# The gates' sigmoid as exp(min(g, 0) - ln(1 + exp(-|g|))) in place of 1 / (1 + exp(-g))

## The chip, the cores and the metric

The kernel runs on one core of one Trainium2 chip. The metric is the device time of one execution in microseconds, all input loads and the output store included. Engines are called as the profile calls them: PE is TensorE (PEld its weight loads), DVE is VectorE, ACT is ScalarE, POOL is GpSimd, SP is SyncE.

## What is computed

A first transformer-like block (Fourier mixing, attention, a gated delta rule, an MLP), and then a second block of two layers. The change lies in the second block's attention, whose core is this:

```
h = x @ w_in[i]                                      # x: 256 tokens x 1024 channels, fp32
(fq, fk, fv, ff_logit, sq, sk, sv, dq, dk, dv, iq, ik, iw, g) = split_cols(h)
o_fox = fox_attention(fq, fk, fv, log_f)             # 6 heads, softmax
o_sb  = stick_breaking_attention(sq, sk, sv)         # 5 heads
o_dsa = dsa_attention(dq, dk, dv, iq, ik, iw)        # 5 heads, softmax over selected keys
gates = jax.nn.sigmoid(g.reshape(b, s, 3, 1024))
merged = (gates[:, :, 0] * (o_fox @ w_up_fox[i])
          + gates[:, :, 1] * (o_sb @ w_up_sb[i])
          + gates[:, :, 2] * (o_dsa @ w_up_dsa[i]))
x = layer_norm(DEEPNORM_ALPHA * x + merged @ w_out[i], ln1_g[i], ln1_b[i])
```

g has 3 x 1024 channels for 256 tokens. Its sigmoid is used only at `merged`, after all heads.

## The kernel before

All products are fp32 on 128 partitions. The second block is a loop over two layers (`second_block`). Each layer is one block of five instruction streams, one per engine, that run in their own written order and meet only at semaphores.

PSUM banks 4 to 7 are used in turn by a list of jobs (`layer_jobs`): job n takes bank 4 + n mod 4, and TensorE may open it once job n - 4 has been read out for the last time. Each job names the engine that gives this last reading ("dve" or "act"). The class `Reader` counts these readings: `open` waits for the job's products (`products_done`), `read` marks the last reading (`dve_emptied` or `act_emptied`). `Writer` does the same on TensorE. `Step` is an engine's wait for its own earlier results.

The order of the attention is written by `attention_schedule()` and followed by all three compute engines. First come eight index heads. Then, for n = 0 to 16, a round of up to four jobs stands: **S** (scores of head n), **T** (of head n - 1: transposed probabilities, or the running sums of a stick-breaking head), **gate n** while n < 12, and **V** (the values' product of head n - 1). Heads 0 to 5 are fox, 6 to 10 stick-breaking (sb), 11 to 15 dsa. So T and V belong to an sb head in the rounds n = 7 to 11, all of which have a gate, and the rounds 12 to 16 have none. As a full round has four jobs, each gate takes the bank of the gate before it.

A gate job is 2 x 8 matmuls of 128x256 with the weights in the ring buffer (line 814), and gives 512 columns: two groups of 128 channels for 256 tokens. The SBUF tensor `sig` holds all twelve.

What the engines do with gate n:

- ScalarE, at gate n: one ACTIVATE from PSUM, exp(-g), into `sig` (line 1086). It is the job's last reading.
- VectorE, at gate n: `sigmoid(n - 1)`, that is 1 + sig (line 1217) and its reciprocal (line 1218) for the gate *before*. The twelfth stands after the last head, ahead of the merge.

In an sb head ScalarE forms ln(1 + exp(-|z|)) by Abs, Exp and Ln (lines 1097, 1099, 1101), VectorE combines it (lines 1246, 1249, 1251), adds T (line 1276), ScalarE takes the Exp (line 1117), and at V VectorE forms the weights (line 1282) before it reads V's product (line 1287). TensorE's V product (lines 969 to 971) waits for these weights (`sb_weights`). In a softmax head VectorE scales and reduces the scores (lines 1258, 1262, 1263), ScalarE takes the Exp and copies T (line 1042), VectorE divides V by its sum (lines 1291, 1292). The selection of keys (lines 1207, 1210) runs on VectorE in the first four fox heads.

After the heads come the transposes of the output (line 979), the up-projections (lines 988 to 995) and the merge on VectorE, which reads `sig` (lines 1305 to 1310).

Of the kernel before, what the change touches and what calls it, by code (L numbers as in the profile page):

```python
# [21 lines left out]
ALU = mybir.AluOpType  # L22
ACT = mybir.ActivationFunctionType
# [262 lines left out]
GATE_JOBS = 12  # L286


def attention_schedule():

    steps = [("idx", str(h)) for h in range(8)]
    last = None
    for n, (kind, h) in enumerate(HEADS + [(None, None)]):
        if kind:
            steps.append(("S", f"{kind}{h}"))
        if last:
            steps.append(("T", last))
        if n < GATE_JOBS:  # L300
            steps.append(("gate", str(n)))
        if last:
            steps.append(("V", last))
        last = f"{kind}{h}"
    return steps


def layer_jobs():
    j = Jobs()
    for c in range(4):  # L310
        j.add(f"xT{c}", "act")
    for n in ("fq01", "fq2fk0"):
        j.add(n, "act")
    j.add("fk12", "dve")
    j.add("ikw", "dve")
    for t in range(TT):
        j.add(f"fv{t}", "dve")
    for n in ("iq01", "iq23"):
        j.add(n, "act")
    for n in ("dq01", "dq2dk"):  # L320
        j.add(n, "act")
    for t in range(TT):
        j.add(f"dv{t}", "dve")
    for n in ("sq01", "sq2sk0", "sk12"):
        j.add(n, "act")
    for t in range(TT):
        j.add(f"sv{t}", "act")
    for n in ("ik", "iq01", "iq23", "dq01", "dq2dk"):
        j.add(f"rot_{n}", "dve")
    j.add("cum", "dve")  # L330
    j.add("cumT", "act")
    for kind, n in attention_schedule():
        j.add(f"{kind}_{n}", {"idx": "act", "gate": "act", "S": "dve", "V": "dve",
                              "T": "dve" if n[:2] == "sb" else "act"}[kind])
    for c in range(4):
        j.add(f"oT{c}", "act")
    for c in range(KC):
        j.add(f"up{c}a", "dve")
        j.add(f"up{c}b", "dve")
    for c in range(4):  # L340
        j.add(f"yT{c}", "act")
    return j


def build(nc, a, out):
# [4 lines left out]
    with ExitStack() as ctx:  # L350
# [35 lines left out]
        def sem(name):  # L386
            return ctx.enter_context(nc.semaphore(name))
# [23 lines left out]
        sb_ln_done, sb_lnot, sb_exp, sb_weights = sem("sb_ln_done"), sem("sb_lnot"), sem("sb_exp"), sem("sb_weights")  # L411
        ik_in, pT_in, bf_in_sem, merged = sem("ik_in"), sem("pT_in"), sem("bf_in"), sem("merged")
        ple_added = sem("ple_added")
        first_sems = [sem(n) for n in ("qk_ready", "g_ready", "conv_ready", "l2_ready", "L_ready", "A_ready", "X_ready",
                                       "vk_ready", "S_zero", "dn_ready", "x1_ready", "gate_in", "conv_out",
                                       "conv_silu", "conv_exp", "e2_done", "decay_in", "decay_done", "pads_zero",
# [7 lines left out]
                     probs_ready, max_ready,  # L424
                     acc_full, out_done, consts_in, hid_full, hid_raw, hid_done, ple_full,
                     ple_exp, ple_read, idx_used, ln_ready, lf_in, lf_ln, lf_ready, sb_ln_done, sb_lnot, sb_exp,
                     sb_weights, ik_in, pT_in, bf_in_sem, merged, ple_added, *first_sems]
        numbers = sorted(s.num for s in loop_sems)
        assert numbers == list(range(numbers[0], numbers[-1] + 1))
        clear = range(numbers[0], numbers[-1] + 1)  # L430
# [248 lines left out]
        def second_block():  # L679
# [8 lines left out]
            sig = carve(24 * SEQ)  # L688
# [49 lines left out]
            with nc.Fori(0, LAYERS) as layer:  # L738
# [11 lines left out]
                with nc.Block() as block:  # L750
# [281 lines left out]
                    def _(act):  # L1032
                        step = Step(act, act_step)
                        r = Reader(act, j2, "act", step)
# [5 lines left out]
                        def copy(name, dst, width=512, scale=None):  # L1040
                            ps = r.open(name, width)
                            ins = act.activation(dst, ps, ACT.Copy) if scale is None else act.mul(dst, ps, scale)  # L1042
                            r.read(name, ins)
# [4 lines left out]
                        ps = r.open("fq2fk0")  # L1048
# [12 lines left out]
                        ps = r.open("dq2dk")  # L1061
# [4 lines left out]
                        ps = r.open("sq2sk0")  # L1066
                        act.mul(sqT[0:HD, 512:768], ps[0:HD, 0:256], 0.125)
                        r.read("sq2sk0", act.activation(skT[:, 0:256], ps[:, 256:512], ACT.Copy))
                        ps = r.open("sk12")
# [4 lines left out]
                        ps = r.open("cumT", 256)  # L1074
                        r.read("cumT", act.activation(cT[0:6, :], ps[0:6, :], ACT.Copy))

                        for kind, name in attention_schedule():
                            if kind == "idx":
                                h = int(name)
                                if h >= 2:  # L1080
                                    act.wait_ge(idx_used, h - 1)
                                r.read(f"idx_{name}", act.activation(rl[h % 2], r.open(f"idx_{name}", 384), ACT.Relu))
                            elif kind == "gate":
                                n = int(name)

                                r.read(f"gate_{n}", act.activation(sig[:, 512 * n:512 * (n + 1)],
                                                                   r.open(f"gate_{n}"), ACT.Exp, scale=-1.0))
                            elif kind == "S":
                                k, h = head(name)[:2]
                                if k == "sb":  # L1090

                                    act.wait_ge(products_done, j2.full(f"S_{name}"))
                                    ps = psum[:, j2.bank(f"S_{name}"), 0:384]
                                    b = sb_ln[h % 2]
                                    if h >= 2:
                                        act.wait_ge(sb_lnot, h - 1)
                                    step(act.activation(b, ps, ACT.Abs))
                                    step.wait()
                                    step(act.activation(b, b, ACT.Exp, scale=-1.0))
                                    step.wait()  # L1100
                                    act.activation(b, b, ACT.Ln, bias=1.0).then_inc(sb_ln_done, 1)
                                else:
                                    i = softmax_heads.index(name)
                                    act.wait_ge(max_ready, i + 1)
                                    if i >= 2:
                                        act.wait_ge(products_done, j2.full(f"T_{softmax_heads[i - 2]}"))
                                    d = 2 * i
                                    act.activation(pr[i % 2][:, 0:P], ts[i % 2][:, 0:P], ACT.Exp,
                                                   bias=nmax[:, d:d + 1], accum_out=den[:, d:d + 1])
                                    act.activation(pr[i % 2][:, P:384], ts[i % 2][:, P:384], ACT.Exp,  # L1110
                                                   bias=nmax[:, d + 1:d + 2],
                                                   accum_out=den[:, d + 1:d + 2]).then_inc(probs_ready, 1)
                            elif kind == "T":
                                k, h = head(name)[:2]
                                if k == "sb":
                                    act.wait_ge(emptied["dve"], j2.emptied(f"T_{name}")[1])
                                    act.activation(sb_arg[h % 2], sb_arg[h % 2], ACT.Exp).then_inc(sb_exp, 1)
                                else:
                                    i = softmax_heads.index(name)
                                    if i >= 2:  # L1120
                                        act.wait_ge(products_done, j2.full(f"V_{softmax_heads[i - 2]}"))
                                    copy(f"T_{name}", pt[i % 2], 384)
                        for c in range(4):
                            copy(f"oT{c}", oT[:, 512 * c:512 * (c + 1)])
                        act.wait_ge(merged, KC)
# [27 lines left out]
                    def _(dve):  # L1153
# [3 lines left out]
                        def do(ins):  # L1157
                            step(ins)
                            step.wait()
# [50 lines left out]
                                    step(dve.match_replace(score[:, at:at + n], best[t], score[:, at:at + n], TAKEN))  # L1210
                                step.wait()

                        def sigmoid(n):

                            r.after(f"gate_{n}")
                            g = sig[:, 512 * n:512 * (n + 1)]
                            do(dve.tensor_scalar(g, g, 1.0, None, ALU.add))
                            step(dve.reciprocal(g, g))  # L1218

                        for kind, name in attention_schedule():  # L1220
                            if kind == "idx":
# [13 lines left out]
                                if h == 7:  # L1235
                                    do(dve.tensor_tensor(score, score, const_a("chunked"), ALU.add))
                            elif kind == "gate":
                                if int(name) > 0:
                                    sigmoid(int(name) - 1)
                            elif kind == "S":  # L1240
                                k, h = head(name)[:2]
                                ps = r.open(f"S_{name}", 384)
# [49 lines left out]
                                    r.read(f"V_{name}", dve.tensor_tensor(dst, v3(ps, HD), spread(rden[:, d:d + 2], HD),  # L1292
                                                                          ALU.mult))
                        step.wait()
                        sigmoid(GATE_JOBS - 1)
                        step.wait()


                        sig4 = sig.rearrange("p (b c t) -> p b c t", b=3, c=KC)
                        for c in range(KC):  # L1300
# [1083 lines left out]
```

## Time and profile before

| | |
|---|---|
| time, median of 3 runs | 1898.52 us (1897.86 to 1905.82) |
| profiled execution: time, span | 1899.21 us, 1897.4 us |
| TensorE busy | 89% of the span, granted clock 0.903 on average |
| VectorE busy | 46%, 871.7 us |
| ScalarE busy | 24%, 458.8 us |
| DMA | 228.75 MB, 121 GB/s on average |

The profile is of one execution, from the hardware's profiler. Its span is the time from the first to the last instruction; the time of the execution holds 1.8 us more. A granted clock of 1.00 is 2.4 GHz, one of 0.50 is 1.2 GHz. The two attention stages, one per layer, lie at about 838 to 991 us and 1432 to 1585 us; the rows below are of the first, and those of the second read alike. An engine's rows are merged where alike instructions follow each other: x32 is 32 records. A matmul in fp32 shows as two records. "[0.28 <-DVE work L1282]" says that the engine was idle for 0.28 us before the row and what ended that.

### The profile page before, as it was taken

What the parts mean: (1) busy time and instruction counts of PE and PEld (TensorE: products, weight loads), DVE (VectorE), ACT (ScalarE), POOL (GpSimd) and SP (SyncE); (2) the same over time, 40 slices, a digit from 0 to 9 for tenths busy, and PEclk for the clock granted to TensorE, in tenths of its full rate; (3) what the DMA queues carried; (4) which work ended last, traced back from release to release, by engine and by line L of the source; (5) the groups of instructions that cost most, each with busy time, mean ns of one, the idle gap of its engine ahead of it and who ended that gap; (6) DMA issues with size and microseconds to landing.
All of it is one profiled execution on the core that took longest, in us unless ns stands there. A gap on an engine that the chain in (4) does not pass through costs nothing. (4 is left out here: it accounts for less than half of the span.)

```text
span 1897.4 us, 22118 instructions
## 1 busy us (share of the span) xinstructions
PE 1690.6 (89%) x8995; PEld 1323.4 (70%) x8995; DVE 871.7 (46%) x1319; ACT 458.8 (24%) x755; POOL 36.8 (2%) x59
## 2 busy tenths in 40 slices
PE   4997989998799979989979899994998988799995
PEld 1555978556499967768865699953776876499982
DVE  0634965333455530047644555543007654455536
ACT  2102232112244420011220344401002221244420
POOL 0002010000000000000000000000000000000000
PEclk7987989675899988989979899996998997999998
DMA  9421110330445216322313454405432231545420
GB/s 361 149 89 46 44 46 1 126 129 13 147 174 200 100 45 208 137 89 89 133 45 119 167 199 179 177 0 180 139 116 89 93 129 45 177 158 196 177 89 22
DMA packets 102156, 228.75 MB, mean 121 GB/s; under 512 B 5441, under 2 KB 13761, under 8 KB 101313
## 3 DMA queue, kind: packets, MB, share of 16 engines
q1 hardware_dynamic: 99056, 219.80, 32.6%
q10 hardware_dynamic: 3024, 7.90, 1.1%
q8 instruction: 54, 0.88, 0.2%
q14 instruction: 22, 0.17, 0.0%
HBM read 226.64 MB, written 1.05 MB: 120 GB/s over the span
## 5 line engine op out<-in xcount | busy, mean ns | idle before, releaser
L814 PE MATMUL psum<-xT,ring 128*128 128x256 f32 (+1 forms) x1504 | 335.8, 386 | 12.9 <-issue 12.9
L814 PEld LDWEIGHTS psum<-xT,ring 128*128 128x128 f32 (+1 forms) x1504 | 273.9, 185 | 66.5 <-issue 18.7
L586 PE MATMUL psum<-channels_rounded,work_rounded 128*128 128x256 f32 x1536 | 284.9, 286 | 2.1 <-DVE work_rounded L654 2.1
L623 DVE TENSOR_TENSOR work_rounded<-ring,work_rounded 128x1024 fp32r<-128x1024 f32 x192 | 222.4, 1220 | 103.9 <-ACT work_rounded L614 103.8
L597 PE MATMUL psum<-work_rounded 128*128 128x512 f32 x1152 | 265.7, 390 | 0.0
L586 PEld LDWEIGHTS psum<-channels_rounded,work_rounded 128*128 128x128 f32 x1536 | 244.9, 195 | 4.8 <-issue 3.9
L597 PEld LDWEIGHTS psum<-work_rounded 128*128 128x128 f32 x1152 | 214.7, 188 | 43.6
L614 ACT ACTIVATE work_rounded<-ring 128x1024 fp32r<-128x1024 f32 x192 | 187.5, 1049 | 176.1 <-PE psum L597 108.3
L586 PE MATMUL psum<-work_rounded 128*128 128x256 f32 x768 | 219.3, 286 | 0.0
L586 PEld LDWEIGHTS psum<-work_rounded 128*128 128x128 f32 x768 | 149.5, 195 | 0.8
L664 DVE TENSOR_TENSOR work<-work 128x512 f32<-128x512 f32 x48 | 33.2, 692 | 110.1 <-ACT work L636 110.1
L1218 DVE RECIPROCAL work<-work 128x512 f32<-128x512 f32 x24 | 80.5, 3354 | 0.8
L1830 ACT ACTIVATE work<-psum 128x512 f32<-128x512 f32 (+1 forms) x65 | 37.5, 577 | 118.1 <-PE psum L1642 85.7
L1042 ACT ACTIVATE work<-psum 128x384 f32<-128x384 f32 (+2 forms) x44 | 22.8, 519 | 174.4 <-PE psum L814 145.5
L636 ACT ACTIVATE work<-psum 128x512 f32<-128x512 f32 x48 | 28.7, 598 | 140.8 <-PE psum L586 140.8
L1498 PE MATMUL psum<-ring,small 128*32 128x512 f32 x192 | 38.2, 939 | 23.8 <-DMA ring<-in_w_mod 23.7
L1001 PE MATMUL psum<-ring,work 128*128 128x512 f32 x128 | 55.5, 594 | 3.0 <-DVE work L1310 3.0
L1027 PE MATMUL psum<-ring,xT 128*128 128x512 f32 x128 | 56.2, 592 | 0.0
L821 PE MATMUL psum<-ring,xT 128*128 128x8 f32 (+3 forms) x256 | 55.1, 369 | 0.0
L821 PEld LDWEIGHTS psum<-ring,xT 128*128 128x128 f32 x256 | 39.8, 196 | 15.4 <-issue 2.3
L666 DVE TENSOR_TENSOR work_rounded<-work,work_rounded 128x512 fp32r<-128x512 f32 x48 | 33.3, 693 | 33.5 <-ACT work_rounded L638 33.5
L1001 PEld LDWEIGHTS psum<-ring,work 128*128 128x128 f32 x128 | 24.2, 190 | 33.5 <-issue 29.7
(353 smaller groups left out, 1969.0 us busy)
## 6 DMA issues: line engine op xcount, KB each, us to landing
ring<-in_w_in SPq DMA_DIRECT2D x22, 2048.0 KB, 8.4
ring<-in_w_ff SPq DMA_DIRECT2D x16, 2048.0 KB, 8.1
ring<-in_w_ff_in SPq DMA_DIRECT2D x16, 2048.0 KB, 7.8
ring<-in_w_ff_out SPq DMA_DIRECT2D x16, 2048.0 KB, 7.8
ring<-in_w_mod SPq DMA_DIRECT2D x12, 2048.0 KB, 8.1
ring<-in_w_out SPq DMA_DIRECT2D x6, 2048.0 KB, 7.9
ring<-in_w_up SPq DMA_DIRECT2D x4, 2048.0 KB, 8.0
ring<-in_w_ple_gate SPq DMA_DIRECT2D x4, 2048.0 KB, 7.8
```

The costliest lines, as they stand in the source:

```text
L586: mm = pe.matmul(psum[:, 4 + 2 * half + q, i * SEQ:(i + 1) * SEQ], w1[pw][:, k, m * P:(m + 1) * P], y[py][:, k, :], start=((k, n) == (0, 0 ...
L597: mm = pe.matmul(psum[:, 2 * t + n, :], h[ph][:, kq, t * P:(t + 1) * P], w2[pw][:, kq, n * 512:(n + 1) * 512], start=False, stop=False, sk ...
L614: act.activation(parts.high[i % 2][:, at], ring[:, SLOT * (n % RING) + 1024 * c: SLOT * (n % RING) + 1024 * (c + 1)], ACT.Copy).then_inc(w ...
L623: dve.tensor_tensor(parts.low[i % 2][:, at], ring[:, SLOT * (n % RING) + 1024 * c: SLOT * (n % RING) + 1024 * (c + 1)], exact(parts.high[i ...
L666: dve.tensor_tensor(parts.h_low[:, 2 * q:2 * q + 2, :], h, exact(parts.h_high[:, 2 * q:2 * q + 2, :]), ALU.subtract).then_inc(hid_done, 1)
L814: mm = pe.matmul(ps[base:base + m, at:at + SEQ], unit[:, k, col:col + m], yT8[:, k, :], start=(k == 0), stop=(k == KC - 1))
L821: mm = pe.matmul(ps[:, at:at + n], yT8[:, k, t * P:(t + 1) * P], unit[:, k, col:col + n], start=(k == 0), stop=(k == KC - 1))
L1001: mm = pe.matmul(psum[:, 2 * t + h, :], mergedT[:, k, t * P:(t + 1) * P], u[:, k, :], start=(k == 0), stop=(k == KC - 1))
L1027: mm = pe.matmul(psum[:, 4 + 2 * t, :], yT8[:, k, t * P:(t + 1) * P], u[:, k, :], start=(k == 0), stop=(k == KC - 1))
L1218: step(dve.reciprocal(g, g))
L1498: mm = pe.matmul(ps[strip, :], cs3[:, k, :], wu[:, k, :], start=(k < 4), stop=(k >= 4))
L1830: r.read(name, act.activation(dst, r.open(name, width), ACT.Copy))
```

## The change

The sigmoid is written as exp(min(g, 0) - ln(1 + exp(-|g|))), which equals 1 / (1 + exp(-g)).

ScalarE takes |g| from PSUM into `sig`, then exp(-|g|) and ln(1 + ...) in place, each behind a wait for the one before. VectorE takes min(g, 0) from PSUM minus that, into `sig`, once `gate_ln` says that the logarithm is there; this is now the job's last reading, so the gate jobs change from "act" to "dve". ScalarE takes the final exp in place one round later (`gate_end`), and `gate_ready` tells VectorE ahead of the merge. The add and the reciprocal go. Per gate ScalarE has four operations where it had one, VectorE one where it had two.

```
-        j.add(f"{kind}_{n}", {"idx": "act", "gate": "act", "S": "dve", "V": "dve",
+        j.add(f"{kind}_{n}", {"idx": "act", "gate": "dve", "S": "dve", "V": "dve",
...
+                        def gate_end(n):
+
+                            g = sig[:, 512 * n:512 * (n + 1)]
+                            r.after(f"gate_{n}")
+                            act.activation(g, g, ACT.Exp).then_inc(gate_ready, 1)
...
                             elif kind == "gate":
                                 n = int(name)
-
-                                r.read(f"gate_{n}", act.activation(sig[:, 512 * n:512 * (n + 1)],
-                                                                   r.open(f"gate_{n}"), ACT.Exp, scale=-1.0))
+                                if n:
+                                    gate_end(n - 1)
+                                g = sig[:, 512 * n:512 * (n + 1)]
+                                step(act.activation(g, r.open(f"gate_{n}"), ACT.Abs))
+                                step.wait()
+                                step(act.activation(g, g, ACT.Exp, scale=-1.0))
+                                step.wait()
+                                act.activation(g, g, ACT.Ln, bias=1.0).then_inc(gate_ln, 1)
...
+                        gate_end(GATE_JOBS - 1)
                         for c in range(4):
                             copy(f"oT{c}", oT[:, 512 * c:512 * (c + 1)])
...
-                        def sigmoid(n):
-
-                            r.after(f"gate_{n}")
+                        def sigmoid_log(n):
+
                             g = sig[:, 512 * n:512 * (n + 1)]
-                            do(dve.tensor_scalar(g, g, 1.0, None, ALU.add))
-                            step(dve.reciprocal(g, g))
+                            ps = r.open(f"gate_{n}")
+                            dve.wait_ge(gate_ln, n + 1)
+                            r.read(f"gate_{n}", dve.scalar_tensor_tensor(out=g, in0=ps, scalar=0.0, in1=g,
+                                                                         op0=ALU.min, op1=ALU.subtract))
...
                             elif kind == "gate":
-                                if int(name) > 0:
-                                    sigmoid(int(name) - 1)
+                                sigmoid_log(int(name))
...
                         step.wait()
-                        sigmoid(GATE_JOBS - 1)
-                        step.wait()
-
+                        dve.wait_ge(gate_ready, GATE_JOBS)
```

Where that puts the instructions, for a round whose T and V are of a stick-breaking head (n = 7, the first of five). On VectorE before, from the add of T (line 1276) over the gate's two operations (1217, 1218) to V's weights (1282), V's copy (1287) and the next head's scores:

```order
L1276 TENSOR_TENSOR work<-work,psum 128x384 [waits dve_emptied,products_done]
L1217 TENSOR_SCALAR work<-work 128x512 [waits act_emptied]
L1218 RECIPROCAL work<-work 128x512 [waits dve_step]
L1282 SCALAR_TENSOR_TENSOR work<-work,shared_consts 128x384 [waits sb_exp]
L1287 COPY work<-psum 128x2x64 [waits products_done,dve_emptied,dve_step]
L1246 SCALAR_TENSOR_TENSOR work<-psum,work 128x384 [waits sb_ln_done,products_done,dve_emptied]
L1249 TENSOR_TENSOR work<-work,shared_consts 128x384 [waits dve_step]
L1251 TENSOR_TENSOR work<-psum,work 128x384
```
On VectorE after, the same stretch; line numbers are those of the changed kernel (1289 is the add of T, 1295 the weights, 1300 V's copy):

```order
L1289 TENSOR_TENSOR work<-work,psum 128x384 [waits dve_emptied,products_done]
L1231 SCALAR_TENSOR_TENSOR work<-psum,work 128x512 [waits gate_ln,products_done,dve_emptied]
L1295 SCALAR_TENSOR_TENSOR work<-work,shared_consts 128x384 [waits sb_exp]
L1300 COPY work<-psum 128x2x64 [waits products_done,dve_emptied]
L1259 SCALAR_TENSOR_TENSOR work<-psum,work 128x384 [waits sb_ln_done,products_done,dve_emptied]
L1262 TENSOR_TENSOR work<-work,shared_consts 128x384 [waits dve_step]
L1264 TENSOR_TENSOR work<-psum,work 128x384
```
In place of the two operations stands one from PSUM (line 1231), which waits for `gate_ln` and for the current gate's products instead of an earlier reading; the weights stand directly behind it.

On ScalarE before, from the Exp of T (line 1117) over the gate's Exp (1086) to the next head's Abs, Exp and Ln:

```order
L1117 ACTIVATE work<-work 128x384 [waits dve_emptied]
L1086 ACTIVATE work<-psum 128x512 [waits products_done,act_emptied]
L1097 ACTIVATE work<-psum 128x384 [waits sb_lnot,products_done]
L1099 ACTIVATE work<-work 128x384 [waits act_step]
L1101 ACTIVATE work<-work 128x384 [waits act_step]
```
On ScalarE after, the same stretch (1129 is the Exp of T, 1082 the final Exp of the gate before, 1095 to 1099 Abs, Exp and Ln of the current gate):

```order
L1129 ACTIVATE work<-work 128x384 [waits dve_emptied]
L1082 ACTIVATE work<-work 128x512 [waits dve_emptied]
L1095 ACTIVATE work<-psum 128x512 [waits products_done]
L1097 ACTIVATE work<-work 128x512 [waits act_step]
L1099 ACTIVATE work<-work 128x512 [waits act_step]
L1109 ACTIVATE work<-psum 128x384 [waits sb_lnot,products_done]
L1111 ACTIVATE work<-work 128x384 [waits act_step]
L1113 ACTIVATE work<-work 128x384 [waits act_step]
```
Four operations stand where one stood. TensorE's order doesn't change; the first matmul of a gate waits for its bank by `dve_emptied` in place of `act_emptied`.

## Rows read from the trace of the kernel before

**Rows 1.** The page: engine shares; costliest groups (busy, mean ns, idle before).

```profile
PE 1690.6 (89%) x8995; PEld 1323.4 (70%) x8995; DVE 871.7 (46%) x1319; ACT 458.8 (24%) x755; POOL 36.8 (2%) x59
...
L1218 DVE RECIPROCAL work<-work 128x512 f32<-128x512 f32 x24 | 80.5, 3354 | 0.8
```
**Rows 2.** Busy time by stretch: PE, PEld, DVE, ACT, POOL; PEclk; DMA share; GB/s.

```profile
862.00:904.00 42.00, 42.00 (x207) 34.63 (x207) 28.50 (x55) 8.42 (x25) 0.00 (x0) 1.00 0.29 100
914.00:962.00 48.00, 46.89 (x236) 40.07 (x235) 31.87 (x39) 12.14 (x25) 0.00 (x0) 1.00 0.25 88
```
**Rows 3.** Timeline of one stick-breaking round (gate 8): start, duration, engine, line.

```profile
923.46 0.49 ACT L1097 ACTIVATE work<-psum 128x384 f32<-128x384 f32 x1 [1.32 <-PE psum L911]
...
923.98 0.52 ACT L1099 ACTIVATE work<-work 128x384 f32<-128x384 f32 x1
...
924.33 7.07 PE L814 MATMUL psum<-xT,ring 128*128 128x256 f32 x32
...
924.54 0.52 ACT L1101 ACTIVATE work<-work 128x384 f32<-128x384 f32 x1
...
925.19 0.56 DVE L1246 SCALAR_TENSOR_TENSOR work<-psum,work 128x384 f32<-128x384 f32 x1 [2.19 <-ACT work L1101]
...
926.84 0.55 DVE L1276 TENSOR_TENSOR work<-work,psum 128x384 f32<-128x384 f32 x1
...
927.77 3.35 DVE L1218 RECIPROCAL work<-work 128x512 f32<-128x512 f32 x1
...
931.04 0.50 DVE L1282 SCALAR_TENSOR_TENSOR work<-work,shared_consts 128x384 f32<-128x384 f32 x1
...
931.50 0.60 ACT L1086 ACTIVATE work<-psum 128x512 f32<-128x512 f32 x1 [3.54 <-PE psum L814]
...
931.68 0.41 PE L969 MATMUL psum<-work 128*128 128x64 f32 x2 [0.28 <-DVE work L1282]
```
**Rows 4.** Groups by line and form, whole execution: count, busy us, mean ns.

```profile
L1920 ACT ACTIVATE work<-work 128x512 f32<-128x512 f32 x8 | 5.0, 630 | 16.6 <-DVE work L2177 16.6
...
L1333 DVE SCALAR_TENSOR_TENSOR x_tok<-x_tok,psum 128x512 f32<-128x512 f32 x8 | 5.5, 688 | 28.0 <-PE psum L1001 28.0
```
**Rows 5.** Timeline: gate 11's end, three rounds of the tail, the merge's start.

```profile
960.90 0.41 PEld L969 LDWEIGHTS psum<-work 128*128 128x128 f32 x2
...
961.38 0.60 ACT L1086 ACTIVATE work<-psum 128x512 f32<-128x512 f32 x1 [5.35 <-PE psum L814]
...
965.58 0.41 PE L969 MATMUL psum<-work 128*128 128x64 f32 x2 [2.36 <-ACT work L1042]
...
970.12 0.66 PE L969 MATMUL psum<-work 128*128 128x64 f32 x2 [2.03 <-ACT work L1042]
...
976.04 0.66 PE L969 MATMUL psum<-work 128*128 128x64 f32 x2 [2.00 <-ACT work L1042]
...
994.66 0.69 DVE L1305 TENSOR_TENSOR work<-psum,work 128x512 f32<-128x512 f32 x1 [3.94 <-PE psum L991]
```
**Rows 6.** Timeline: end of gates 1, 5, 6 and start of 2, 6, 7.

```profile
862.94 0.60 ACT L1086 ACTIVATE work<-psum 128x512 f32<-128x512 f32 x1 [4.74 <-PE psum L814]
...
865.74 0.30 PEld L814 LDWEIGHTS psum<-xT,ring 128*128 128x128 f32 x2
...
903.25 0.60 ACT L1086 ACTIVATE work<-psum 128x512 f32<-128x512 f32 x1 [4.79 <-PE psum L814]
...
904.82 0.30 PEld L814 LDWEIGHTS psum<-xT,ring 128*128 128x128 f32 x2
...
912.10 0.60 ACT L1086 ACTIVATE work<-psum 128x512 f32<-128x512 f32 x1 [5.47 <-PE psum L814]
...
914.26 0.30 PEld L814 LDWEIGHTS psum<-xT,ring 128*128 128x128 f32 x2
```
**Rows 7.** Busy time by stretch around the longest pause before the attention's heads.

```profile
832.40:838.30 5.90, 0.06 (x2) 0.06 (x2) 5.49 (x12) 0.00 (x0) 0.00 (x0) 0.65 0.44 165
838.30:844.20 5.90, 5.90 (x35) 5.07 (x36) 3.00 (x9) 3.04 (x7) 0.00 (x0) 0.50 0.00 0
844.20:850.00 5.80, 5.80 (x28) 4.43 (x26) 5.55 (x18) 2.25 (x7) 0.00 (x0) 0.98 0.00 0
```

More of the change, by code:

```diff
@@ L413, in build @@
         ple_added = sem("ple_added")
+        gate_ln, gate_ready = sem("gate_ln"), sem("gate_ready")
         first_sems = [sem(n) for n in ("qk_ready", "g_ready", "conv_ready", "l2_ready", "L_ready", "A_ready", "X_ready",
@@ L426, in build @@
                      ple_exp, ple_read, idx_used, ln_ready, lf_in, lf_ln, lf_ready, sb_ln_done, sb_lnot, sb_exp,
-                     sb_weights, ik_in, pT_in, bf_in_sem, merged, ple_added, *first_sems]
+                     sb_weights, ik_in, pT_in, bf_in_sem, merged, ple_added, gate_ln, gate_ready, *first_sems]
         numbers = sorted(s.num for s in loop_sems)
```

## The prediction

> **What bounds the kernel now.** I read the engine shares first, then the table by stretch, then the order of time inside one attention round. TensorE is busy in 89% of the span, VectorE in 46%, and the 24 reciprocals that go are 80.5 us of VectorE's time [rows 1]. The stretches say whether those 80.5 us cost anything: in the softmax rounds TensorE is busy 42.00 of 42 us, in the stick-breaking rounds 46.89 of 48, both at full clock [rows 2]. So while the gates run, TensorE is the bound, and a reciprocal is worth only the time by which it makes TensorE wait. A round in time [rows 3] shows how little that is. The 16 gate products (32 records) run from 924.33 for 7.07 us. Beneath them VectorE does the previous head's add (926.84), the gate's add and the reciprocal (927.77), and then the weights of that head's V product (line 1282, from 931.04), which TensorE needs right after the gate. It waits 0.28 us for them. That happens in four rounds a layer, so removing every reciprocal can give back about 8 x 0.28 = 2.2 us.
>
> **What the change does to the order.** It moves the gate's step on VectorE from work on the *previous* gate, done long ago, to work on the *current* gate: VectorE now waits for gate n's products and for three ScalarE operations on them, and only then comes to what stands behind, the previous head's V step. In the rounds n = 7 to 11 that step begins with the weights (line 1282 before, 1295 after), and TensorE's V product, next in its queue after gate n, waits for them. Before, they were made under the gate's products. Now they can't start until these have ended. That is a new wait on the bounding engine.
>
> **Its length.** ScalarE starts on gate n when the products are seen to be done (931.50 in [rows 3]); I count from there. The chain of the same kind exists in the stick-breaking heads at 384 columns: Abs 923.46, Exp 923.98, Ln 924.54, VectorE 925.19 [rows 3]. So an operation takes its own time plus 0.03 us to the next on ScalarE, and plus 0.13 us to VectorE. At 512 columns, the first from PSUM is 0.60 (the ACTIVATE at 931.50), the two on SBUF 0.63 each (line 1920, [rows 4]). Chain: 0.60 + 0.03 + 0.63 + 0.03 + 0.63 + 0.13 = 2.05 us. VectorE's new subtraction reads PSUM at 512 columns, 0.69 (line 1333, [rows 4]); the next independent instruction starts some 0.1 before its end, at 2.65. The weights take 0.50 (931.04), the signal to TensorE about 0.12, and V starts at 3.27.
>
> Rounds 7 to 10: before, V started 0.18 after ScalarE's start (931.68 against 931.50), now 3.27, so +3.09; eight of them over two layers, 24.7 us. Round 11 had no wait: V's weights were loaded 0.48 *before* ScalarE's start (960.90 against 961.38, [rows 5]), so +3.75, twice, 7.5 us. Together 32.2. Everything behind V (the next scores, T, the next gate) shifts with it. None of it is late anew, since after the pause ScalarE and VectorE still have the next 7.07 us of gate products to finish in.
>
> **The bank.** All gates share one PSUM bank, and gate n+1 may begin only when gate n has been read for the last time. That was the Exp, at 0.60; now it is VectorE's subtraction, at 2.05 + 0.69 + 0.15 = 2.9. The next gate began 2.80 after ScalarE's start in the softmax rounds, 1.57 at the change to stick-breaking (gate 6) and 2.16 at gate 7 [rows 6]. So four gates lose 0.1 each, gate 6 loses 1.3, gate 7 0.7: 2.4 a layer, 4.8 in all. In gates 8 to 11 the pause above covers it.
>
> **What hides.** ScalarE gets three more operations of 0.6 us a gate. The final Exp of gate n-1 stands ahead of the wait for gate n, where ScalarE idled 3.54 us before 931.50 [rows 3]. Softmax rounds: VectorE reaches the next scores about 1 us later, with the eight-element searches behind them, but the copy of T that TensorE needs is ScalarE's last work before the gate, and ScalarE then idled 4.74 us (the ACTIVATE at 862.94, [rows 6]). If that cover went, each round would lose at most that 1 us. The last sigmoid, after the final head, is removed from VectorE. It gives nothing: VectorE then idled 3.94 us for TensorE's first up-projection [rows 5].
>
> **The clock.** The ten pauses are 3.75 us long with nothing for TensorE to do (from 0.48 before ScalarE's start to 3.27 after). In the softmax heads behind the gates, pauses of 2.36 us stand between short products. After the first of them (965.58) the same pair of V products goes from 0.41 to 0.66 us [rows 5]: the granted clock went to its lower level. After a stretch of 5.90 us with next to no product, ahead of the heads, the clock was 0.50 (1.2 of 2.4 GHz) for another 5.90 us in which TensorE was busy throughout [rows 7]. No row shows a pause of 3.75 us amid dense products, so a pause's price in clock is bounded from both sides. It is 0 if the 7 us of dense gate products around it hold the level. At most it is 5.90 us at half rate, 2.95 us lost. A middle price comes from the tail: one round of it took 4.54 us at full and 5.92 at the lower clock (965.58, 970.12, 976.04), a loss of 1.38 in 5.92, or 1.4 in a stretch of 5.9. I take 2.5, near the upper end, because what follows a pause here is V, S, T and gate products back to back, while the tail is half waits. Eight times is 20. The pauses of round 11 run into the tail, which is slow already; they bring its fall forward by a round (1.4) and slow the three small steps before it (about 1.0): 2.4, twice, 4.8. Together 24.8.
>
> The Trainium skill's page "TensorE: Matmul & The Clock Gate", section "Wait — 56ns, not 53.3ns?", says that back-to-back matmuls take twice the spacing at 1.2 GHz. By that rule a stretch of 5.9 us would cost 2.95 and the total would come to 1964. The trace here agrees with the doubling only in part (0.41 to 0.66, in products with few columns).
>
> By the tail's round alone, 1.4 a pause, the total would be 1952.
>
> **Sum.** 32.2 + 4.8 + 24.8 = 61.8 us; the 2.2 us given back by line 1282's old wait is already in the 3.09. Against the profiled execution's own 1899.2 that is 1961.0. The median of the runs is 0.7 lower, so 1960.
>
> **Rivals.**
> *The clock holds.* Pauses of 3.75 us among 7 us of dense work leave it at full: only 37.0 us are added, 1935. For it: the stick-breaking rounds are far denser than the tail. Against it: 2.36 us sufficed there, and the pause is longer than half of what comes between.
> *The clock doesn't recover in a gate.* If it stays low through each round, the gate's 7.07 us and the 2.7 us around it double: about 9 more in eight rounds in place of 2.5, 1898.5 + 37 + 72 + 5 = 2012. Against it: after the longer pause in [rows 7] it was back 5.90 us later.
> *Not slower.* Place: VectorE between the gate's step and line 1282. If V's weights were ready when the gate ends, because the Ln signal came before VectorE needs it, the 0.28 us waits would vanish and nothing replace them: -2.2 us, 1896. It decides once the three ScalarE operations and the subtraction fit ahead of the gate's end. They can't, since they read its result; only an order other than the built one would save it.
> *The change doesn't act where it says*, the pause being covered by another wait on TensorE: then 1898. Against it: TensorE is busy 46.89 of 48 us there, so there is no other wait to hide in.
>
> **How the numbers follow.** Forecast 0.70, clock holds 0.17, clock stays low 0.08, unchanged 0.03, faster 0.02. The range takes in the first two. Below, it is 1935 less 0.3 us a pause for the chain; above, 2.95 instead of 2.5 a pause (+3.6) and up to 1 us more per pause for chain and wake-up (+10): 1932 to 1974. A measurement of this kernel tells about 0.5%, 9.5 us, from no change; all cases but the last two are slower by more, so faster 0.02, same 0.03, slower 0.95.
>
> **What would show it.** In the profile after: TensorE's V product (line 970) waiting for VectorE's line 1295 about 3 us in ten places, 30 us in total; VectorE's line 1231 idle before, waiting for ScalarE's Ln; the first gate product waiting for line 1231 some 1.3 and 0.7 us twice each. The stretch of the stick-breaking rounds should show a granted clock well below 1.00. If it is 1.00 there, the clock term is wrong; if line 970 doesn't wait, the main term is. Reciprocals on VectorE at 512 columns fall by 24, and the span isn't shorter for it.

## The result

The changed kernel takes 1960.3 us (median of 4 runs, 1954.5 to 1966.39), the kernel before 1899.17 us: a ratio of 1.0315, 95% interval 1.0275 to 1.0355. It was predicted slower, at 1960 us, within 1932 to 1974 (the kernel before was timed once more beside it, so its median has moved from 1898.52). The profiled execution of the changed kernel is the longest of its four, 1966.39 us with a span of 1964.6, 67.2 us over the span of before; what follows adds up to that.

The page of the changed kernel. The first line gives busy time and share of each engine, the second a group of instructions (line, engine, operation, shape, count, busy us and mean ns, idle time before and what ended it):

```profile
PE 1726.4 (88%) x8995; PEld 1348.1 (69%) x8995; DVE 800.0 (41%) x1295; ACT 501.4 (26%) x827; POOL 36.8 (2%) x59
...
L1231 DVE SCALAR_TENSOR_TENSOR work<-psum,work 128x512 f32<-128x512 f32 x24 | 16.6, 692 | 159.4 <-ACT work L1099 152.4
```

VectorE did lose 72 us of work against [rows 1], and nothing came of it. In its place stands idle time: the new subtraction (line 1231) waited 152.4 us for ScalarE's Ln, and TensorE's V product (line 970), as the next view shows, 33.9 us for VectorE's weights (line 1295), where it had waited 2.2 us in all.

TensorE's waits, summed over the execution (total, times, longest), show the same pause ten times, and the four waits for the PSUM bank:

```profile
PE psum L970 <- DVE work L1295: 33.9, 10, 3.4
...
PE psum L815 <- DVE work L1231: 2.6, 4, 1.0
```

Busy time by stretch (PE, PEld, DVE, ACT, POOL busy, then the granted clock), four softmax and four stick-breaking rounds, to be held against [rows 2]:

```profile
866.00:908.00 42.00, 41.35 (x203) 33.80 (x201) 15.27 (x50) 16.57 (x40) 0.00 (x0) 1.00 0.31 107
918.00:980.00 62.00, 48.08 (x190) 39.94 (x190) 16.13 (x34) 17.15 (x31) 0.00 (x0) 0.83 0.19 68
```

The softmax rounds are as they were, but for 0.65 us at the end of the stretch, where gate 6 waits for its bank. The stick-breaking ones take 62 us where they took 40, with TensorE idle for 14 of them and the clock at 0.83 in place of 1.00.

One stick-breaking round in order of time, gate 8's end to gate 9's start, answers to [rows 3]. Columns: start, duration, engine, line:

```profile
941.41 0.60 ACT L1095 ACTIVATE work<-psum 128x512 f32<-128x512 f32 x1 [4.33 <-PE psum L815]
942.04 0.63 ACT L1097 ACTIVATE work<-work 128x512 f32<-128x512 f32 x1
942.70 0.63 ACT L1099 ACTIVATE work<-work 128x512 f32<-128x512 f32 x1
943.46 0.69 DVE L1231 SCALAR_TENSOR_TENSOR work<-psum,work 128x512 f32<-128x512 f32 x1 [7.46 <-ACT work L1099]
944.07 0.55 DVE L1295 SCALAR_TENSOR_TENSOR work<-work,shared_consts 128x384 f32<-128x384 f32 x1
...
944.76 0.41 PE L970 MATMUL psum<-work 128*128 128x64 f32 x2 [3.39 <-DVE work L1295]
...
945.00 0.61 PE L971 MATMUL psum<-work 128*128 128x64 f32 x2
...
949.41 8.28 PE L815 MATMUL psum<-xT,ring 128*128 128x256 f32 x32
```

The chain of five is laid bare while TensorE waits 3.39 us; V starts 3.35 us after ScalarE's start on the gate. Behind the pause V's second pair of matmuls (line 971, line 970 before) takes 0.61 us where it took 0.39 in the same round before (at 931.92), and the next gate's products take 8.28 us instead of 7.07: the clock fell. By the trace each of the ten pauses brought it to 0.50 once.

**Where the 67.2 us are.** I read the starts of the gates' first products and of the output's transposes (before: line 979, after: line 980) off the timelines.

| stretch | before | after, layer 1 | after, layer 2 |
|---|---|---|---|
| gate 0 to gate 7 | 68.16, 68.17 | 69.91 | 71.60 |
| each round, gate 7 to gate 11 | 9.96 | 15.45 to 15.70 | 15.45 to 15.72 |
| the four rounds | 39.84, 39.83 | 62.29 | 62.45 |
| gate 11 to the transposes | 32.84, 32.92 | 39.53 | 39.50 |
| more than before | | +30.9 | +32.6 |

The two attention stages hold 63.5 of the 67.2 us. In layer 2, 1.7 of them are a stretch of low clock among the softmax rounds, which no wait explains (gate 0 to 7 took 69.91 us in layer 1); the last section comes back to it. The other 3.7 lie outside, 2.3 of them ahead of the first gate, where the program is the same; the timed runs of both kernels scatter by more (1897.9 to 1905.8 and 1954.5 to 1966.4).

### The profile page after: what moved, and what is told of

The parts are those of the page before. It is cut to its first block and busy times, and to the rows that moved or that the text cites. A ratio compares the mean times of both kernels' runs of the same rounds, so it can differ in the third digit from the quotient of the medians.

```text
span 1964.6 us, 22180 instructions
## 1 busy us (share of the span) xinstructions
PE 1726.4 (88%) x8995; PEld 1348.1 (69%) x8995; DVE 800.0 (41%) x1295; ACT 501.4 (26%) x827; POOL 36.8 (2%) x59
## 5 line engine op out<-in xcount | busy, mean ns | idle before, releaser
L815 PE MATMUL psum<-xT,ring 128*128 128x256 f32 (+1 forms) x1504 | 344.6, 393 | 13.1 <-issue 9.7
L815 PEld LDWEIGHTS psum<-xT,ring 128*128 128x128 f32 (+1 forms) x1504 | 280.7, 190 | 69.9 <-issue 15.7
L1231 DVE SCALAR_TENSOR_TENSOR work<-psum,work 128x512 f32<-128x512 f32 x24 | 16.6, 692 | 159.4 <-ACT work L1099 152.4
L970 PE MATMUL psum<-work 128*128 128x64 f32 x64 | 15.6, 334 | 51.4 <-DVE work L1295 33.9
L970 PEld LDWEIGHTS psum<-work 128*128 128x128 f32 x64 | 13.3, 241 | 59.5 <-DVE work L1231 37.6
```

What stands on the lines that cost most here:

```text
L815: mm = pe.matmul(ps[base:base + m, at:at + SEQ], unit[:, k, col:col + m], yT8[:, k, :], start=(k == 0), stop=(k == KC - 1))
L970: pe.matmul(ps[:, 0:HD], pb[:, 0:P], v[:, 0, vc:vc + HD], start=True, stop=True)
```

## The experiments

The kernel before was timed again beside each group of runs, and each run is compared with that time. "More" is the ratio less one, times the median of the kernel before, since the interval belongs to the ratio; the plain difference of the medians can lie up to 2.4 us away from it.

### One instruction earlier

The changed kernel, with V's weights formed ahead of the gate's subtraction:

```
+                        def weights(n):
+
+                            if 6 <= n < 11:
+                                dve.wait_ge(sb_exp, n - 5)
+                                b = sb_arg[(n - 6) % 2]
+                                dve.scalar_tensor_tensor(out=b, in0=b, scalar=-1.0, in1=const_a("sb_neg"),
+                                                         op0=ALU.mult, op1=ALU.mult).then_inc(sb_weights, 1)
...
                             elif kind == "gate":
+                                weights(int(name) - 1)
                                 sigmoid_log(int(name))
...
-                                if k == "sb":
-                                    dve.wait_ge(sb_exp, h + 1)
-                                    b = sb_arg[h % 2]
-                                    dve.scalar_tensor_tensor(out=b, in0=b, scalar=-1.0, in1=const_a("sb_neg"),
-                                                             op0=ALU.mult, op1=ALU.mult).then_inc(sb_weights, 1)
```

> The changed kernel with one instruction moved: in the five stick-breaking rounds VectorE forms the weights of the previous head's V ahead of the gate's subtraction, where it stood idle. All arithmetic of the change stays. Theory (the cost is the order: V's weights queued behind a wait for the current gate): the ten waits of TensorE's V product for VectorE vanish, and with them the fall of the clock in these rounds, 56 of the 61 us. What stays is the bank that is free only at 2.9 us after ScalarE's start (about 1.9 us a layer up to gate 7, 0.3 in each of gates 8 to 11) and some 1.6 us at the start of the tail, where the first scores of the dsa heads are read behind the subtraction: 9 us in all, 1908 us. Rival (the three added operations a gate and the second reading of PSUM cost by themselves): 1935 or more.

Measured: 1914.74 us (6 runs) beside 1901.58 for the kernel before, ratio 1.0068 (1.0044 to 1.0092), about 13 us more than before. The waits of V for VectorE are gone from the list of TensorE's waits. Its stick-breaking rounds last 10.01 us each, at full clock:

```profile
917.00:957.00 40.00, 38.84 (x192) 33.42 (x192) 14.85 (x30) 16.69 (x31) 0.00 (x0) 1.00 0.30 105
```

So one instruction's place in VectorE's queue carried about 48 of the 61 us (56 were expected), with all arithmetic of the change still there. What stays is 13 us, 4 more than the 9 expected. Gate 0 to 7 took 69.91 us in layer 1 (+1.75), as expected, and the four rounds 0.05 more each, where I had expected 0.3. The tail took 35.90 instead of 32.84, +3.1 against the expected 1.6: the dsa scores are read behind the subtraction, TensorE waits longer for what follows from them, and the clock is low a round earlier. The timeline of the first round of the tail:

```profile
966.54 0.69 DVE L1239 SCALAR_TENSOR_TENSOR work<-psum,work 128x512 f32<-128x512 f32 x1 [5.73 <-ACT work L1099]
...
967.59 0.56 DVE L1280 SCALAR_TENSOR_TENSOR work<-psum,work 128x384 f32<-128x384 f32 x1
...
970.33 0.66 PE L970 MATMUL psum<-work 128*128 128x64 f32 x2 [3.94 <-ACT work L1043]
```

TensorE idles 3.94 us here, in [rows 5] it was 2.36, and the product behind is already slow (0.66). In layer 2 one stretch of low clock among the softmax rounds adds 1.7 us; that is taken up at the end.

### The old arithmetic in the new place

The kernel before, its add and reciprocal for gate n moved to gate n:

```
                             elif kind == "gate":
-                                if int(name) > 0:
-                                    sigmoid(int(name) - 1)
+                                sigmoid(int(name))
...
-                        sigmoid(GATE_JOBS - 1)
```

> The kernel before with the order of the change: VectorE's add and reciprocal of gate n at gate n, in place of one gate later; ScalarE and all arithmetic as before. Theory (order): V now waits for 0.60 Exp + 0.13 + 0.42 add + 3.35 reciprocal + 0.50 weights + signal, so it starts 5.15 us after ScalarE's start in place of 0.18: 8 x 5.0 + 2 x 5.6 = 51 us of waits, and 25 to 32 us of clock, 1975 to 1982 us. The bank is free as early as before, so the first seven gates cost nothing. Rival (the new form's operations are what costs): 1899 us.

Measured: 1984.0 us beside 1901.58, ratio 1.0435 (1.0404 to 1.0467), 83 us more, at the upper end of the expected 76 to 83. The waits sum to the expected 51 us, in ten alike of 5.1 instead of eight of 5.0 and two of 5.6 (the 5.6 were counted from V's earlier start in round 11):

```profile
PE psum L969 <- DVE work L1281: 51.0, 10, 5.1
```

Gate 0 to 7 took 68.17 us in layer 2, as before, and 69.85 in layer 1, where one stretch of low clock lies. No operation of the change is in this kernel, and it is slower still. Only the order does that; the cheaper arithmetic of the change softens the wait from 5.1 us to 3.4.

### The pause filled

The changed kernel with eight matmuls of no use behind gates 7 to 11:

```
+FILL = 8
...
                                 w.done(channels(ps, SEQ, u, (2 * (n % 2) + 1) * P, P))
+                                if n >= 7:
+                                    for k in range(FILL):
+                                        pe.matmul(psum[:, 0, 0:SEQ], yT8[:, k, 0:P], yT8[:, k, :],
+                                                  start=(k == 0), stop=(k == FILL - 1))
```

> The changed kernel with eight 128x256 matmuls of no use (into a bank that is free then) behind the gate in rounds 7 to 11, 3.5 us of products inside the 3.8 us pause, on data that is there anyway. The waits for V's weights end when they did. Theory (20 to 25 of the 61 us are the clock that falls in the pauses): the granted clock stays at 1.00 in the rounds, only the waits are left, about 37 us over the kernel before, 1936 us. Rival (the clock has no share and the waits are longer than I read them): 1960 us, as without the matmuls.

Measured: 1941.01 us (1939.82 to 1943.78) beside 1901.58, ratio 1.0205 (1.0176 to 1.0234), 39 us more where 37 were expected. TensorE does *more* work than in the changed kernel and the kernel is some 20 us faster. The stretch of the rounds, and one pause in order of time:

```profile
920.00:972.00 52.00, 51.74 (x252) 44.43 (x253) 15.16 (x32) 17.04 (x31) 0.00 (x0) 1.00 0.24 81
```

```profile
940.34 3.62 PE L940 MATMUL psum<-xT 128*128 128x256 f32 x16
940.54 0.60 ACT L1100 ACTIVATE work<-psum 128x512 f32<-128x512 f32 x1 [2.97 <-PE psum L816]
...
943.20 0.55 DVE L1300 SCALAR_TENSOR_TENSOR work<-work,shared_consts 128x384 f32<-128x384 f32 x1
...
943.89 0.41 PE L975 MATMUL psum<-work 128*128 128x64 f32 x2
```

V starts 3.35 us after ScalarE, exactly as without the filling (943.89 against 940.54), so the wait is untouched. The clock is 1.00, and a round takes 13.07 us. That splits the changed kernel's round, 15.57 us in the mean of layer 1's four: 9.96 before, 3.11 for the wait, and 15.57 - 13.07 = 2.5 us for the clock.

### One pause a layer, and two

The new form for chosen gates only, the others as before:

```
+NEW = [9]
...
+                                if n not in NEW:
+                                    r.read(f"gate_{n}", act.activation(g, r.open(f"gate_{n}"), ACT.Exp, scale=-1.0))
+                                    continue
...
+                                n = int(name)
+                                if n and n - 1 not in NEW:
+                                    sigmoid(n - 1)
+                                if n in NEW:
+                                    sigmoid_log(n)
...
```

> The new form for gate 9 alone, the eleven others as before, so one pause a layer. Theory: the pause costs 3.17 us of wait and 2.45 of clock each, as one round of the changed kernel costs, 2 x 5.6 = 11 us, 1910 us. Rival (the pauses bring the clock down only together, one among dense rounds is free of that): 2 x 3.2 = 6 us, 1905 us.

Measured: 1915.18 us beside 1901.58, ratio 1.0059 (1.0034 to 1.0084), 11.2 us more (13.6 by the medians) where the theory had 11; the interval (6.5 to 16) excludes the rival only just. The trace is needed. Gate 9 to gate 11 took 24.20 and 24.25 us in the two layers, two rounds. The second of them is an old round without its 0.28 us wait, since no reciprocal precedes its weights, and lasts 9.44 us at full clock (the last experiment below measures that). So the wait and the two rounds make 9.96 + 3.11 + 9.44 = 22.51, and the clock's share is 1.7 us in either layer, not 2.45, and not nothing. When I wrote the expectation of the next run I took 9.96 for the second round and came to 1.2; 1.7 is right. So the time met the theory in part by luck: the pair of rounds grew by 4.3 us in each layer, not by 5.6, but the tail took 34.22 and 33.75 us instead of 32.84 and 32.92, as the clock stayed low in it for 30.7 us instead of 23.9, and layer 1 has a stretch of low clock in the softmax rounds besides.

The same with `NEW = [7, 9]`:

> The new form for gates 7 and 9 alone, the others as before: four pauses in all, each with an undisturbed round behind it. The clock's share of the lone pauses at gate 9 was 1.2 us, in the row of pauses it was 2.45. Theory A (a pause's clock share depends on where it falls in the chip's watch over TensorE, so it varies from pause to pause): shares between 1.2 and 2.9 us, unlike each other, the lower clock lasting about 3.4 or about 6.8 us. Theory B (a lone pause costs less since the products before it are dense): 1.2 us at each of the four, the lower clock never over 3.4 us. In time: A 19 to 24, B 17 us over the kernel before.

Measured: 1925.78 us beside 1900.67, ratio 1.0123 (1.0081 to 1.0164), 23.4 us more, in theory A's range (the medians differ by 25.1); the interval (15 to 31) doesn't exclude B by itself. The trace does. The four pairs of rounds took 25.84, 25.22, 24.20 and 25.89 us, a clock share of 3.3, 2.7, 1.7 and 3.4. The lower clock lasted 6.83 us in three of them and 3.41 in one:

```profile
926.74:933.57 6.83, 6.83 (x19) 5.55 (x19) 2.99 (x6) 2.58 (x5) 0.00 (x0) 0.50 0.47 178
1534.31:1537.72 3.41, 3.41 (x12) 2.80 (x11) 0.81 (x3) 1.54 (x3) 0.00 (x0) 0.50 0.78 297
```

TensorE is busy throughout both, so half of each is lost: 3.4 and 1.7 us. In the pair that lost 2.7 the low stretch (6.83 us from 950.63) began 1.2 us before V did (951.84), so part of it fell into the wait. The pauses are alike (3.45 us of wait each), and their price in clock differs by two: behind gate 7 it was 3.3 us in layer 1 and 1.7 in layer 2, with the same code, and behind gate 9 it was 2.7 and 3.4 here but 1.7 twice in the one-pause kernel. Theory B is out. That the price hangs on when a pause falls, theory A's reason, fits this but was not tested by itself. The mean of 2.5 in the changed kernel is a mean of such prices.

### The softmax rounds alone

The same form with `NEW` = gates 0 to 6, the rest as before.

> The new form for gates 0 to 6 alone, gates 7 to 11 as before, so no pause for V's weights is left. Theory (the bank): gates 6 and 7 start 1.1 and 0.6 us later than before, the softmax gates 2 to 5 as before or within 0.1, 1.9 us a layer, 3.7 us over the kernel before. Rival (twelve more operations on ScalarE and the later reading of the scores in the softmax rounds cost something of their own): over 8 us more than before.

Measured: 1906.59 us (10 runs) beside 1900.67, ratio 1.0022 (1.0000 to 1.0045), 4.2 us more (0 to 8.5; 5.9 by the medians), where 3.7 were expected and the rival began at 8. The waits for the bank are those of the changed kernel:

```profile
PE psum L816 <- DVE work L1243: 2.6, 4, 1.0
```

Gate 0 to 7 took 69.91 us in layer 1, +1.75, the bank's share. The three more ScalarE operations per gate and the later reading of the scores, here in seven gates, cost nothing else in these rounds. In both layers the tail took 34.2 us instead of 32.8 or 32.9, with the clock low for 27.3 us instead of 23.9, though its code is that of the kernel before; the four rounds ahead of it were together 0.4 us shorter. Layer 2 has the stretch of low clock too (71.59 us for gate 0 to 7).

### The kernel before, its weights first

The same move as in the first experiment, made in the kernel before:

```
...
                             elif kind == "gate":
+                                weights(int(name) - 1)
                                 if int(name) > 0:
                                     sigmoid(int(name) - 1)
...
```

> The kernel before with one instruction moved: VectorE forms the stick-breaking weights of the previous head's V ahead of the gate's add and reciprocal. Theory: the reciprocals reached the path only by the eight waits of 0.28 us, so these vanish and nothing else changes: 2.2 us less than before, at most. Rival (VectorE's reciprocals hold TensorE up in some other place, so that moving them brings more): over 5 us less.

Measured: 1901.85 us (12 runs) beside 1900.67, ratio 0.9996 (0.9976 to 1.0016), no difference that the runs can tell; the interval, -4.6 to +3.0 us, excludes the rival but still holds the expected -2.2. The trace shows two effects that were not expected. The four rounds behind gate 7 fell from 9.96 to 9.44 us, more than the 0.28 each that the wait's row showed. In the kernel before, TensorE's weight loader stood idle for 0.65 us ahead of V and loaded V's weights when the gate's products were over; here it loads them under the gate's last products, 0.4 us before these end. The two rows, before and here:

```profile
931.65 0.30 PEld L969 LDWEIGHTS psum<-work 128*128 128x128 f32 x2 [0.65 <-issue]
...
929.89 0.41 PEld L969 LDWEIGHTS psum<-work 128*128 128x128 f32 x2
```

That is 2.1 us a layer. But the tail grew from 32.84 to 34.06: the low clock lasted 30.7 us there instead of 23.9. Net 0.8 us a layer. No version tried beats the kernel before, and this is the one whose time lies nearest to it.

## Why the prediction was right, point by point

**The pause for V's weights: right in cause, place, number and size.** 32.2 us were predicted (3.09 in eight rounds, 3.75 in two), and the filled pause measures the first as 3.11. The chain ran to the letter: 2.05 us from ScalarE's start to VectorE's (943.46 - 941.41), the weights 0.61 later. They took 0.55 us instead of the 0.50 that the row had right behind a reciprocal; where VectorE had been idle ahead of them, in the two kernels with the weights first, they took 0.56. V started at 3.35 against the 3.27 of the sum. The rows that gave this were of another chain, at 384 columns, and of other lines at 512 [rows 3, 4], and they served.

**The bank: right in place, a third too large.** 2.4 us a layer predicted, 1.75 measured in the changed kernel and alone. Gates 2 to 5 lost nothing (10.08 us apart before and after) where I had put 0.1 each. For VectorE to release the bank I had added 0.15 us to the subtraction's end, and it took 0.05: in the changed kernel it starts at 907.56, ends at 908.25, and TensorE's gate 6 starts at 908.30:

```profile
907.56 0.69 DVE L1231 SCALAR_TENSOR_TENSOR work<-psum,work 128x512 f32<-128x512 f32 x1 [7.63 <-ACT work L1099]
908.30 0.73 PEld L815 LDWEIGHTS psum<-xT,ring 128*128 128x128 f32 x4 [1.20 <-DVE work L1231]
```

**The clock: right in size, as a mean, and in part by luck.** 2.5 us a pause were chosen, not worked out, between bounds of 0 and 2.95, and 15.57 - 13.07 = 2.5 were measured in the row of pauses. The single ones cost 1.7 to 3.4, so the upper end of 2.95 was too low for one pause: the low stretch lasts up to 6.8 us, not 5.9. The 5.90 was only the width chosen for the stretches of [rows 7]; the trace has the clock at 0.50 from 834.16 to 844.40, 6.1 us past the end of that pause. The rule of twice the spacing at the lower clock, from the Trainium skill's page "TensorE: Matmul & The Clock Gate", section "Wait — 56ns, not 53.3ns?", agrees with these traces for back-to-back products: a stretch of 6.83 us costs 3.4, half of it. The tail's round was a poor guide. Of its 5.92 us 2.0 are waiting, a third, not half; and the round of 4.54 us to which it was compared as one at full clock ran at the lower clock from 967.28 on, so the loss of 1.38 was read too small. In the tail, gate 11 to the transposes, 3.75 + 2.4 = 6.15 us were predicted and 6.6 to 6.7 measured.

**What hides: right, for the softmax rounds ahead of the tail.** ScalarE's three operations more and the scores read a microsecond later cost nothing in gates 0 to 5 (10.08 us apart). At the start of the tail the late reading does lengthen a wait once the pause is gone (3.94 us for 2.36, first experiment); in the changed kernel no wait in the tail is over 2.0 us. The last sigmoid's removal gave nothing that shows; it wasn't tested alone. The 2.2 us that the reciprocals had cost weren't gained, since the same product now waits longer.

**The rivals.** "The clock holds" (1935) is what the filled pause shows: 1941 where the kernel before took 1901.6. In the changed kernel it fell, as the objection from the 2.36 us pause had it. "The clock doesn't recover" was not seen: no low stretch in a round lasted over 6.83 us in the changed kernel, and 10.2 with the 5.1 us pauses of the old arithmetic. "Not slower" fails on the order alone, as the second experiment shows. The prediction called 2.2 us the most that the reciprocals can give back; the last experiment found 4.1 in the rounds, of which the tail took 2.4 back.

The sum met the median, 1960.3, closer than its terms deserve: against the sum the bank came out 1.3 us lower and the tail 1 us higher, and layer 2 has 1.7 us of low clock that no term had.

## What to carry to other kernels

An engine at 46% can still be the one that everybody waits for, if an instruction that the bounding engine needs stands in its queue behind a wait for that engine's newest result. Before shortening an engine's work, write down what stands behind each new wait in its queue and who waits for that; here it was one instruction, and moving it up gave back about 48 of 61 us. A pause of TensorE among dense products was paid for twice here, once as idle time (3.1 us) and once, nearly as dearly, in the clock behind it (2.5 us in the mean).

## What the runs showed of the hardware

- Each of the ten pauses (3.4 us without products, 3.8 without weight loads) brought the granted clock from 2.4 to 1.2 GHz, and where dense rounds followed it returned after 3.4 or 6.8 us. Behind the lone pauses the work lost 1.7 to 3.4 us, not the same each time.
- Products of no use in the pause kept the clock at 1.00, and the kernel was some 20 us faster for more work on TensorE.
- The clock also fell without a pause. In five of the nine profiles it went to 0.50 for 3.4 us in one layer's softmax rounds, where the trace shows TensorE busy throughout (in the one-pause kernel 14.45 of the 14.45 us before the fall), and in the one-pause kernel the code of these rounds is the same as before's. That stretch of it:

```profile
869.45:872.86 3.41, 3.41 (x11) 2.78 (x10) 3.27 (x14) 1.36 (x5) 0.00 (x0) 0.50 1.03 393
```

  It came behind the run of short products of V, S and T (64 to 256 columns) between two gates in all five, cost 1.7 us (here 11.63 us for 10.08 in the round it lay in, and 0.13 in the one before), and I haven't found what decides it.
- A short wait cost TensorE more than its row says: without 0.28 us of waiting the round was 0.52 us shorter.
